# The beginning of a two-layer diffusion kernel: first three scales on TensorE, another order of loads, low parts right behind their products

## The chip, the core and the metric

One core of a Trainium2 chip runs the whole program in one launch. TensorE (PE) multiplies, VectorE (DVE), ScalarE (ACT) and GpSimd (POOL) work elementwise, SyncE (SP) issues the loads. The metric is the device time of one launch in microseconds, lower is better.

## What is computed

Three transformer blocks of width 1024 run over 256 latent and 256 context tokens, with nine condition vectors per layer made from silu(c). The change touches only the first half-FFN of the first layer, whose input is a modulated norm:

```python
def adaln(cond, w, b):
    m = jax.nn.silu(cond) @ w + b
    return m.reshape(m.shape[:-1] + (N_MOD, D_MODEL))

def modulated_norm(h, g, m, k):
    return rmsnorm(h, g) * (1.0 + m[..., k + 1, :]) + m[..., k, :]

def half_ffn(h, m, k, g_pre, g_post, w_in, w_out):
    y = swiglu(modulated_norm(h, g_pre, m, k), w_in, w_out)
    return gated_residual(h, y, g_post, m, k, 0.5)
```

Here k is 0: the shift is m[0], the scale m[1]. There are two conditions, one for the context tokens and one for the latents.

## The kernel before

Activations are held transposed: 1024 channels are 8 chunks (CH) of 128 partitions, with all 512 tokens along the free axis. Every weight product is made of three single-pass products of 512 columns (or 256): w_hi x u_hi, w_lo x u_hi and w_hi x u_lo, so weights and activations are both split in a high part (rounded to fp32r) and a low part (what the rounding left). `head` (L802) on ScalarE makes w_hi of a weight tile, `rest` (L779) on GpSimd makes w_lo, in four quarters for the tiles of the beginning. Weight tiles (128 x 1024, 512 KB) sit in a ring of 6; a new one is loaded when `tile_used` says that one has been used.

The beginning, up to the first 96 products, runs so. SyncE (L702 on) issues, in order: the transposed condition silu_t (small), h in two halves, weight tile 0, the spread condition silu_c (every partition holds both conditions, 1 MB), the small columns col, and then for each chunk c a scale tile, a shift tile (512 KB each) and the next weight tile; then tables. ScalarE (L837 on) takes silu of silu_t, squares h chunk by chunk, then in `first_norm` (L875) takes silu of silu_c, loads the table of exp and log, makes 1/rms (`rstd`) when the sum of squares is there, and for each chunk adds the bias to the shift (mcol), makes u_hi for the two halves of the tokens and a head. VectorE (L1136 on) adds up the squares, makes two small sums for a later block (lam), and in `first_norm` (L1295) does for each chunk: two dot products of the scale tile with silu_c (`dot`, L1150), a_col = (1 + scale) times gain, v = h x a_col x rstd for both halves (`v_part`), and `u_low` of the chunk before it. TensorE waits in `start_phase` (L1726): one matmul with ones for the sum of squares, then for each chunk a `shift(c)` (8 fp32 matmuls of a shift tile with the two columns of silu_t, 16 records in a trace), and `run(tile, k)`, the three products of one weight tile with chunk k, for four weight tiles and 8 chunks, 96 products in all. u_lo is waited for just before the third product of a `run`.

Two dots are junk-written to psum banks 0 and 1; shift sums are in banks 6 and 7. After the 96 products `ffn_body` goes on with pair after pair of weight tiles over all 8 chunks, and nothing in the rest of the program waits for anything of the beginning but through those products, u, and the ring.

`keep_clock(bank, count)` (L1645) issues `count` fp32 matmuls of ones with 128 columns, two records each; before the change the beginning doesn't call it, later stages do.

Of the kernel before, what the change touches and what calls it, by code (L numbers as in the profile page):

```python
# [14 lines left out]
D = 1024  # L15
# [353 lines left out]
def build(nc, A):  # L369
# [106 lines left out]
    cond_in, tables_in, consts_in, dist_in = sem("cond_in"), sem("tables_in"), sem("consts_in"), sem("dist_in")  # L476
    h_in = [sem("h_low_in"), sem("h_high_in")]
# [40 lines left out]
    FIRST_DOTS = 2 * CH  # L518
# [175 lines left out]

    def exps_through(kind, U):
        return (2 if kind == "da" else 1) * (U + 1)
# [6 lines left out]
    def _(sp):  # L703
        sp.dma_start(silu_t[:, :, :], A["cond_t"]).then_inc(cond_in, 16)
        for i in range(2):
            c = slice(4 * i, 4 * i + 4)
            sp.dma_start(h[:, c, :], A["hT"][:, c, :]).then_inc(h_in[i], 16)

# [89 lines left out]
    def _(act):  # L798
# [76 lines left out]
        def first_norm(b):  # L875
            heads_to(0)
            act.wait_ge(consts_in, 32)
            scalar.activation(silu_c[:, :, :], silu_c[:, :, :], ACT.Silu).then_inc(silu_c_ready, 1)
            scalar.preload_act_table_set(EXP_SET)
            act.wait_ge(set_up, 2)  # L880
            act.wait_ge(first_sum, CH)
# [3 lines left out]
            heads_to(1)  # L885
            for c in range(CH):
                act.wait_ge(shift_sum, c + 1)
                bias = COL["ada_b"] + c
                scalar.activation(mcol[:, :, c:c + 1], psum[:, SUMS + c % 2, 0:2].rearrange("p (c o) -> p c o", o=1),
# [4 lines left out]
                heads_to(min(c + 2, 5))  # L894
# [232 lines left out]
    def _(dve):  # L1127
# [15 lines left out]
        dve.wait_ge(consts_in, 32)  # L1143
        for m in range(2):
            l0 = COL["lambda"] + 2 * m * DA_QK
            vec.tensor_tensor_reduce(out=lam_t[:, m, :], in0=col[:, l0:l0 + DA_QK], in1=col[:, l0 + DA_QK:l0 + 2 * DA_QK],
                                     scale=1.0, scalar=0.0, op0=ALU.mult, op1=ALU.add,
                                     accum_out=small[:, 2 + m:3 + m]).then_inc(lam_sum, 1)

# [145 lines left out]
        def first_norm(b):  # L1295

            one_more, g = stat[:, 0, :], COL["norm_g"]
            bias = COL["ada_b"] + CH
            vec.tensor_scalar(one_more, col[:, bias:bias + CH], 1.0, None, ALU.add).then_inc(scale_step, 1)
            dve.wait_ge(scale_step, 1)  # L1300
            dve.wait_ge(silu_c_ready, 1)
# [287 lines left out]
    def _(pe):  # L1589
# [136 lines left out]
        def start_phase(b, tiles):  # L1726

            pe.wait_ge(silu_t_ready, 1)
            pe.wait_ge(first_sum, CH - 1)
            mm(psum[:, SUMS, :], ones[:, :], sq_first[:, CH - 1, :], start=True, stop=True).then_inc(first_sum, 1)  # L1730

            def shift(c):
                pe.wait_ge(shift_in[c], 16)
                if c == 0:
# [3 lines left out]
                for k in range(CH):  # L1738
                    last = mm(psum[:, SUMS + c % 2, 0:2], first_tile(CH + c)[:, k * 128:(k + 1) * 128], silu_t[:, k, :],
                              start=k == 0, stop=k == CH - 1)  # L1740
                last.then_inc(shift_sum, 1)
# [385 lines left out]
```

## Time and profile before

| | us |
|---|---|
| median of 3 runs (lowest, highest) | 2386.48 (2383.85, 2388.22) |
| the profiled execution, its own time | 2385.69 |
| its span, first to last instruction | 2383.9 |
| PE busy / weight loads busy | 2313.7 (97%) / 2067.1 (87%) |
| DVE / ACT / POOL busy | 1306.3 / 974.4 / 1340.7 |

Time outside the span is 1.8 us. A busy PE means that matmuls are in flight, not that the array is at its peak; PEclk is the clock granted to TensorE as a share of full speed (1.0 is 2.4 GHz, 0.5 is 1.2 GHz), and it is told as 1.00 where no record of the clock exists yet, as at the very beginning. There the duration of a matmul tells the clock. Rows of a timeline give the start, the time, the engine, the source line and what the engine waited for.

### The profile page before, as it was taken

Reading aid. Unit: us, or ns where it says so; the run is one execution under the profiler, and the core shown is the slowest. Engines: PE = TensorE matmul, PEld = TensorE weight load, DVE = VectorE, ACT = ScalarE, POOL = GpSimd, SP = SyncE. Lnnn points to the kernel's source line nnn. Section 1 sums busy time; section 2 is a strip of 40 time slices with the busy share of each in tenths; the row PEclk is TensorE's granted clock in tenths of the full one; section 3 lists DMA queues with packets and bytes.
Section 4 is the critical chain, followed back from the end, with each engine's and each line's share of the span. In section 5 each row is a group of like instructions: output and inputs, shape, how many; then the busy total and the mean of one; then the engine's idle time right before and its main releaser. Section 6 shows DMA issues by size and latency. Waiting matters only on the chain.

```text
span 2383.9 us, 36103 instructions
## 1 busy us (share of the span) xinstructions
PE 2313.7 (97%) x14528; PEld 2067.1 (87%) x14528; DVE 1306.3 (55%) x2196; ACT 974.4 (41%) x1605; POOL 1340.7 (56%) x700
## 2 busy tenths in 40 slices
PE   7999999999889999999999998999999999999998
PEld 5888889777688888898888897799999999999998
DVE  8898296666678982967332126554324315533331
ACT  4332224455443322234222235555444444555443
POOL 4554465222234554654544443278879887468886
PEclk9999999999999999999999999999999999999999
DMA  6555362211025553534453332145645564345554
GB/s 271 212 180 191 111 219 86 71 53 63 27 80 206 176 193 119 213 101 177 175 193 109 96 91 79 45 160 186 179 154 190 181 185 161 108 151 184 185 178 134
DMA packets 97508, 350.09 MB, mean 147 GB/s; under 512 B 10944, under 2 KB 10944, under 8 KB 96960
## 3 DMA queue, kind: packets, MB, share of 16 engines
q1 hardware_dynamic: 97344, 347.81, 43.6%
q8 instruction: 115, 1.88, 0.3%
q14 instruction: 49, 0.40, 0.1%
HBM read 346.71 MB, written 1.05 MB: 146 GB/s over the span
## 4 chain that ended last, share of the span: by engine, by line
PE 47%; DVE 3%; ACT 2%; POOL 1%; issue 1%; DMA 1%; DVEq 0%; ACTq 0%
PE psum L1601 15%; PE psum L1605 15%; PE psum L1602 15%; POOL w_lo L786 1%; PE psum L1950 1%; ACT w_hi L806 1%; PE psum L1922 0%; PE psum L1930 0%; DVE stat L1517 0%; PE psum L1912 0%; DVE u_lo L1457 0%; DMA w_raw<-in_ga_in 0%; ACT prob L1067 0%; DVE sbias L1508 0%; DVE psum L1233 0%
## 5 line engine op out<-in xcount | busy, mean ns | idle before, releaser
L786 POOL TENSOR_TENSOR w_lo<-w_raw,w_hi 128x1024 fp32r<-128x1024 f32 (+3 forms) x696 | 1340.5, 1948 | 1026.2 <-ACT w_hi L806 1025.6
L1601 PE MATMUL psum<-u_hi,w_hi 128*128 128x256 f32 (+2 forms) x2912 | 973.3, 334 | 11.9 <-POOL w_lo L786 7.8
L1605 PE MATMUL psum<-u_lo,w_hi 128*128 128x256 f32 (+2 forms) x2912 | 949.3, 326 | 3.8 <-DVE u_lo L1225 2.0
L1602 PE MATMUL psum<-u_hi,w_lo 128*128 128x256 f32 (+2 forms) x2912 | 946.9, 325 | 0.0
L806 ACT ACTIVATE w_hi<-w_raw 128x1024 fp32r<-128x1024 f32 (+1 forms) x522 | 537.4, 1032 | 439.2 <-PE psum L1605 345.9
L1601 PEld LDWEIGHTS psum<-u_hi,w_hi 128*128 128x128 f32 x2912 | 554.9, 191 | 75.1 <-issue 24.3
L1605 PEld LDWEIGHTS psum<-u_lo,w_hi 128*128 128x128 f32 x2912 | 554.1, 190 | 52.6 <-DVE u_lo L1225 4.9
L1602 PEld LDWEIGHTS psum<-u_hi,w_lo 128*128 128x128 f32 x2912 | 555.0, 191 | 45.9 <-issue 3.1
L1601 PE MATMUL psum<-gu_hi,w_hi 128*128 128x256 f32 (+1 forms) x1188 | 379.3, 319 | 0.1
L1602 PE MATMUL psum<-gu_hi,w_lo 128*128 128x256 f32 (+1 forms) x1188 | 378.1, 318 | 0.0
L1605 PE MATMUL psum<-gu_lo,w_hi 128*128 128x256 f32 (+1 forms) x1188 | 378.1, 318 | 0.0
L1601 PEld LDWEIGHTS psum<-gu_hi,w_hi 128*128 128x128 f32 x1188 | 226.3, 191 | 16.2 <-issue 0.5
L1602 PEld LDWEIGHTS psum<-gu_hi,w_lo 128*128 128x128 f32 x1188 | 226.3, 191 | 15.7
L1605 PEld LDWEIGHTS psum<-gu_lo,w_hi 128*128 128x128 f32 x1188 | 226.3, 191 | 15.3
L1153 DVE CUSTOM_DVE_ANT_0 psum<-ada_hi,silu_c,col 128x1024 f32<-128x1024 f32 x80 | 155.2, 1940 | 55.6 <-DMA ada_hi<-in_ada_w 52.0
L960 ACT ACTIVATE sq<-psum 128x512 f32<-128x512 f32 x66 | 39.5, 598 | 326.3 <-PE psum L1605 176.0
L1153 DVE CUSTOM_DVE_ANT_0 psum<-ada_lo,silu_c,col 128x1024 f32<-128x1024 f32 x80 | 144.9, 1812 | 30.9 <-DMA ada_lo<-in_ada_w 26.3
L1330 DVE TENSOR_TENSOR gu_lo<-sq,gu_hi 128x512 fp32r<-128x512 f32 (+1 forms) x132 | 147.4, 1117 | 17.4 <-ACT gu_hi L945 17.3
L1362 DVE TENSOR_TENSOR sq<-sq,psum 128x512 f32<-128x512 f32 (+1 forms) x110 | 63.6, 578 | 166.1 <-PE psum L1605 161.0
L1249 DVE TENSOR_TENSOR rstd<-rstd,sq 128x256 f32<-128x256 f32 (+1 forms) x58 | 46.1, 794 | 180.9 <-ACT sq L904 89.0
L1153 DVE CUSTOM_DVE_ANT_0 psum<-ada_out,silu_c,col 128x1024 f32<-128x1024 f32 x64 | 132.8, 2136 | 0.1
L1067 ACT ACTIVATE prob<-psum,stat 128x512 f32<-128x512 f32 (+1 forms) x80 | 47.6, 599 | 103.9 <-DVE stat L1519 103.8
(180 smaller groups left out, 1988.9 us busy)
## 6 DMA issues: line engine op xcount, KB each, us to landing
w_raw<-in_ffn_in SPq DMA_DIRECT2D x264, 512.0 KB, 3.5
w_raw<-in_ffn_out SPq DMA_DIRECT2D x96, 448.0 KB, 3.4
ada_hi<-in_ada_w SPq DMA_DIRECT2D x48, 512.0 KB, 5.1
ada_lo<-in_ada_w SPq DMA_DIRECT2D x48, 512.0 KB, 5.2
w_raw<-in_ffn_out SPq DMA_DIRECT2D x48, 512.0 KB, 3.6
ada_out<-in_ada_w SPq DMA_DIRECT2D x32, 512.0 KB, 3.8
w_raw<-in_b_qkv SPq DMA_DIRECT2D x30, 512.0 KB, 3.5
w_raw<-in_da_in SPq DMA_DIRECT2D x24, 512.0 KB, 3.4
```

The source lines that it names most:

```text
L786: last = pool.tensor_tensor(w_lo[:, slot, w], w_raw[:, slot, w], w_hi[:, slot, w].bitcast(F32), ALU.subtract)
L806: scalar.activation(w_hi[:, slot, 0:cols], w_raw[:, slot, 0:cols], ACT.Copy).then_inc(hi_ready, 1)
L960: scalar.activation(s_up[:, j, tok], psum[:, pair_bank(m), tok], ACT.Silu).then_inc(silu_ready, 1)
L1067: scalar.activation(prob[:, U % 2, m * 512:m * 512 + n], src, ACT.Exp, bias=stat[:, U % 4, 2 + m:3 + m], scale=scale, accum_out=stat[:, U ...
L1153: return vec.tensor_tensor_reduce(out=psum[:, junk:junk + 2, :].rearrange("p a b -> p (a b)"), in0=tile, in1=silu_c[:, c, :], scale=1.0, s ...
L1249: vec.tensor_tensor(sqsum[:, tok], sqsum[:, tok], sq[:, i % 2, tok], ALU.add).then_inc(yacc_ready, 1)
L1330: vec.tensor_tensor(gu_lo[:, m, tok], s_up[:, m % 2, tok], gu_hi[:, m, tok].bitcast(F32), ALU.subtract)\
L1362: vec.tensor_tensor(s_up[:, j, tok], s_up[:, j, tok], psum[:, pair_bank(m) + 1, tok], ALU.mult)\
L1601: mm(out, w_hi[:, slot, w], x_hi, start=start and n == 0, stop=False)
L1602: mm(out, w_lo[:, slot, w], x_hi, start=False, stop=False)
L1605: last = mm(out, w_hi[:, slot, w], x_lo, start=False, stop=stop and n == len(ks) - 1)
L1950: last = mm(psum[:, pv_bank(kind, st["s"], half), x["ocol"]:x["ocol"] + 128], v_tile(st["v"][g], kt), probT[:, U % 2, n * 128:(n + 1) * 12 ...
```

## The change

On TensorE: `start_phase` begins with 32 matmuls of `keep_clock`, sums the squares in four matmuls of pairs (with one more `keep_clock` matmul between them) in place of one, makes the scales of chunks 0, 1 and 2 with matmuls as the shifts are made (`condition`), and runs the products in another order. On VectorE: the adds of squares are four pair adds in place of a chain of seven, the dots of chunks 0 to 2 are gone (a_col is made from psum), each `u_low` stands behind the `v_part` of its own chunk, and the two dots of the next chunk stand one before and one behind it. On ScalarE: the exp table is loaded right behind the first silu and the silu table behind rstd, silu of silu_c is done in two halves behind u_hi of chunk 2, and heads come at other places. SyncE loads what the new order uses first, and silu_c behind the tiles of chunk 2. The table load at the head of the first `ffn_body` falls away. (A few lines of loads that the diff adds behind the `return` of `lag_of` are never reached.)

```diff
@@ names and constants @@
+    silu_in, first_pair, scale_sum = sem("silu_in"), sem("first_pair"), sem("scale_sum")
...
+    BY_PE = 3
+    FIRST_DOTS = 2 * (CH - BY_PE)
...
@@ SyncE: the loads @@
+        def load_scale(c):
+
+            source = A["ada_shift"][CH + c] if c < BY_PE else A["ada_w"][CH + c]
+            sp.dma_start(first_tile(c), source).then_inc(scale_in[c], 16)
+
+        def load_shift(c):
+
+            sp.dma_start(first_tile(CH + c), A["ada_shift"][c]).then_inc(shift_in[c], 16)
...
         load(A["ffn_in0"][0], 0)
-        sp.dma_start(silu_c[:, :, :], A["cond"]).then_inc(consts_in, 16)
         sp.dma_start(col[:, :], A["columns"]).then_inc(consts_in, 16)
-        for c in range(CH):
-            sp.dma_start(first_tile(c), A["ada_w"][CH + c]).then_inc(scale_in[c], 16)
-            sp.dma_start(first_tile(CH + c), A["ada_shift"][c]).then_inc(shift_in[c], 16)
-            if c + 1 < RING:
-                load(A["ffn_in0"][c + 1], c + 1)
+        for c in range(2):
+            load_scale(c)
+            load_shift(c)
+        for t in range(1, 4):
+            load(A["ffn_in0"][t], t)
+        for c in range(2, CH):
+            load_scale(c)
+            load_shift(c)
+            if c == 2:
+                sp.dma_start(silu_c[:, :, :], A["cond"]).then_inc(silu_in, 16)
+            if c > 5:
+                load(A["ffn_in0"][c - 2], c - 2)
         sp.dma_start(tab[:, :], A["tables"]).then_inc(tables_in, 16)
...
@@ ScalarE @@
         scalar.activation(silu_t[:, :, :], silu_t[:, :, :], ACT.Silu).then_inc(silu_t_ready, 1)
+        scalar.preload_act_table_set(EXP_SET)
...
             heads_to(0)
-            act.wait_ge(consts_in, 32)
-            scalar.activation(silu_c[:, :, :], silu_c[:, :, :], ACT.Silu).then_inc(silu_c_ready, 1)
-            scalar.preload_act_table_set(EXP_SET)
             act.wait_ge(set_up, 2)
-            act.wait_ge(first_sum, CH)
+            act.wait_ge(first_sum, 1)
             rstd_of(rstd[:, :], psum[:, SUMS, :], 1.0 / D, first_rstd)
             act.wait_ge(lam_sum, 2)
             scalar.activation(small[:, 4:6], small[:, 2:4], ACT.Exp).then_inc(lam_exp, 1)
-            heads_to(1)
+            scalar.preload_act_table_set(SILU_SET)
+            act.wait_ge(consts_in, 16)
             for c in range(CH):
                 act.wait_ge(shift_sum, c + 1)
                 bias = COL["ada_b"] + c
-                scalar.activation(mcol[:, :, c:c + 1], psum[:, SUMS + c % 2, 0:2].rearrange("p (c o) -> p c o", o=1),
+                scalar.activation(mcol[:, :, c:c + 1], psum[:, RSTD - c % 2, 0:2].rearrange("p (c o) -> p c o", o=1),
...
-                heads_to(min(c + 2, 5))
+                heads_to((2, 3, 3, 3, 3, 3, 4, 5)[c])
+                if c == BY_PE - 1:
+                    act.wait_ge(silu_in, 16)
+                    for i in range(2):
+                        scalar.activation(silu_c[:, i, :], silu_c[:, i, :], ACT.Silu).then_inc(silu_c_ready, 1)
...
@@ VectorE @@
-        for c in range(1, CH):
-            dve.wait_ge(first_sq, c + 1)
-            if c > 1:
-                dve.wait_ge(first_sum, c - 1)
-            total = psum[:, RSTD, :]
-            vec.tensor_tensor(sq_first[:, c, :] if c == CH - 1 else total, sq_first[:, 0, :] if c == 1 else total,
-                              sq_first[:, c, :], ALU.add).then_inc(first_sum, 1)
...
+            for x in (0, 2, 4, 6):
+                dve.wait_ge(first_sq, x + 2)
+                vec.tensor_tensor(sq_first[:, x + 1, :], sq_first[:, x, :], sq_first[:, x + 1, :], ALU.add)\
+                   .then_inc(first_pair, 1)
...
+            def scale_dot(c, i):
+
+                if c < BY_PE or c >= CH:
+                    return
+                if c == BY_PE:
+                    dve.wait_ge(silu_c_ready, i + 1)
+                dve.wait_ge(scale_in[c], 16)
+                dot(first_tile(c), i, 2 * (c - BY_PE) + i, 0, ada_sum[:, c % 2, i:i + 1], 0)
+
             for c in range(CH):
-                dve.wait_ge(scale_in[c], 16)
-                for i in range(2):
-                    dot(first_tile(c), i, 2 * c + i, 0, ada_sum[:, c % 2, i:i + 1], 0)
-                dve.wait_ge(ada_dot, 2 * c + 2 + ADA0)
-                vec.tensor_scalar(a_col[:, 0:6:3, c:c + 1], ada_sum[:, c % 2, :].rearrange("p (c o) -> p c o", o=1),
+                if c < BY_PE:
+                    dve.wait_ge(scale_sum, c + 1)
+                    scale = psum[:, c % 2, 0:2]
+                else:
+                    dve.wait_ge(ada_dot, 2 * (c - BY_PE) + 2 + ADA0)
+                    scale = ada_sum[:, c % 2, :]
+                vec.tensor_scalar(a_col[:, 0:6:3, c:c + 1], scale.rearrange("p (c o) -> p c o", o=1),
                                   one_more[:, c:c + 1], col[:, g + c:g + c + 1], ALU.add, ALU.mult)\
...
                     v_part(b, p, tok, c, rstd)
-                    if c:
-                        u_low(b, p, tok, c - 1)
-            for p, tok in enumerate(halves(FULL)):
-                u_low(b, p, tok, CH - 1)
+                scale_dot(c + 1, 0)
+                for p, tok in enumerate(halves(FULL)):
+                    u_low(b, p, tok, c)
+                scale_dot(c + 1, 1)
...
@@ TensorE @@
+            keep_clock(PVB, 32)
+            for n in range(4):
+                pe.wait_ge(first_pair, n + 1)
+                last = mm(psum[:, SUMS, :], ones[:, :], sq_first[:, 2 * n + 1, :], start=n == 0, stop=n == 3)
+                if n < 3:
+                    keep_clock(PVB, 1)
+            last.then_inc(first_sum, 1)
             pe.wait_ge(silu_t_ready, 1)
-            pe.wait_ge(first_sum, CH - 1)
-            mm(psum[:, SUMS, :], ones[:, :], sq_first[:, CH - 1, :], start=True, stop=True).then_inc(first_sum, 1)
...
+            def scale(c):
+
+                pe.wait_ge(scale_in[c], 16)
+                if c == 2:
+                    pe.wait_ge(scale_step, 2)
+                condition(first_tile(c), psum[:, c % 2, 0:2]).then_inc(scale_sum, 1)
...
+            scale(0)
             shift(0)
+            scale(1)
+            run(*tiles[0], 0)
+            shift(1)
+            scale(2)
+            run(*tiles[0], 1)
             for k in range(2):
-                shift(k + 1)
-                for tile in tiles[:2]:
-                    run(*tile, k)
+                run(*tiles[1], k)
+            shift(2)
             for k in range(2):
-                for tile in tiles[2:]:
-                    run(*tile, k)
-            for k in range(2, CH):
+                run(*tiles[2], k)
+            for tile in tiles[:3]:
+                run(*tile, 2)
+            shift(3)
+            for k in range(3):
+                run(*tiles[3], k)
+            for k in range(3, CH):
                 if k + 1 < CH:
                     shift(k + 1)
                 for tile in tiles:
...
@@ the tensors made on the host @@
-    X["ada_shift"] = I["ada_w"][0][:, 0:D].reshape(CH, 128, CH, 128).transpose(2, 1, 0, 3).reshape(CH, 128, D)
+    X["ada_shift"] = I["ada_w"][0][:, 0:D + 384].reshape(CH, 128, CH + 3, 128).transpose(2, 1, 0, 3).reshape(CH + 3, 128, D)
```

## Rows read from the trace of the kernel before

**Rows 1.** Windows: busy us (instructions) of each engine, granted clock, DMA share, GB/s.

```profile
0.00:13.23 13.23, 0.00 (x0) 0.03 (x1) 5.07 (x9) 6.82 (x11) 1.27 (x6) 1.00 0.83 324
18.19:25.02 6.83, 6.83 (x33) 6.83 (x33) 6.69 (x10) 3.02 (x5) 5.82 (x6) 1.00 1.02 408
25.02:28.79 3.77, 3.07 (x7) 1.97 (x8) 3.73 (x6) 2.23 (x4) 3.66 (x4) 1.00 1.03 412
32.06:37.05 4.99, 4.78 (x11) 3.29 (x12) 4.89 (x8) 2.23 (x4) 2.74 (x4) 1.00 1.03 410
37.05:50.80 13.75, 13.61 (x84) 11.76 (x83) 13.53 (x23) 4.11 (x10) 5.85 (x6) 1.00 0.39 156
50.80:54.20 3.40, 3.40 (x9) 2.62 (x10) 3.29 (x7) 0.37 (x1) 0.00 (x0) 0.50 0.00 0
54.20:66.47 12.27, 12.27 (x72) 10.68 (x71) 9.73 (x21) 4.67 (x9) 0.00 (x0) 1.00 0.06 15
66.47:150.00 83.53, 83.53 (x370) 69.19 (x369) 76.50 (x75) 24.00 (x32) 49.65 (x16) 1.00 0.60 214
150.00:320.00 170.00, 170.00 (x752) 140.77 (x751) 112.84 (x124) 48.22 (x61) 80.25 (x31) 1.00 0.46 161
```

**Rows 2.** Timeline of TensorE: sum of squares, shifts (L1739), products (L1601, L1602, L1605).

```profile
13.23 2.04 PE L1730 MATMUL psum<-sq_first,ones 128*128 128x512 f32 x2 [13.23 <-DVE sq_first L1141]
18.19 6.96 PE L1739 MATMUL psum<-silu_t,first_b 128*128 128x2 f32 x32 [2.92 <-ACT rstd L834]
...
26.92 0.80 PE L1605 MATMUL psum<-u_lo,w_hi 128*128 128x512 f32 x1 [0.70 <-DVE u_lo L1225]
...
28.79 3.41 PE L1739 MATMUL psum<-silu_t,first_b 128*128 128x2 f32 x16
...
35.35 0.63 PE L1601 MATMUL psum<-u_hi,w_hi 128*128 128x512 f32 x1
35.77 0.63 PE L1602 MATMUL psum<-u_hi,w_lo 128*128 128x512 f32 x1
...
38.97 1.84 PE L1739 MATMUL psum<-silu_t,first_b 128*128 128x2 f32 x16
40.67 0.47 PE L1601 MATMUL psum<-u_hi,w_hi 128*128 128x512 f32 x1
...
43.52 1.84 PE L1739 MATMUL psum<-silu_t,first_b 128*128 128x2 f32 x16
...
50.65 0.67 PE L1605 MATMUL psum<-u_lo,w_hi 128*128 128x512 f32 x1
```

**Rows 3.** Timeline of VectorE: lambda sum, dots (L1153) of chunks 2, 6 and 7.

```profile
13.48 0.23 DVE L1146 CUSTOM_DVE_ANT_0 lam_t<-col 128x64 f32<-128x64 f32 x1 [0.39 <-DMA col<-in_columns]
...
26.79 1.76 DVE L1153 CUSTOM_DVE_ANT_0 psum<-first_a,silu_c 128x1024 f32<-128x1024 f32 x1
...
50.52 1.22 DVE L1153 CUSTOM_DVE_ANT_0 psum<-first_a,silu_c 128x1024 f32<-128x1024 f32 x1
...
55.07 1.22 DVE L1153 CUSTOM_DVE_ANT_0 psum<-first_b,silu_c 128x1024 f32<-128x1024 f32 x1
```

**Rows 4.** Timeline of ScalarE: squares, silu of silu_c, rstd, mcol, u_hi.

```profile
8.95 2.19 ACT L843 ACTIVATE sq_first<-h 128x512 f32<-128x512 f32 x4 [0.38 <-DMA h<-in_hT]
...
13.48 1.91 ACT L878 ACTIVATE silu_c<-silu_c 128x2048 f32<-128x2048 f32 x1 [1.39 <-DMA col<-in_columns]
15.40 1.28 ACT L879 ACT_TABLE_LOAD   x1
16.70 0.69 ACT L826 ACTIVATE rstd<-psum,small 128x512 f32<-128x512 f32 x1
...
21.78 0.26 ACT L889 ACTIVATE mcol<-psum,col 128x2 f32<-128x2 f32 x1 [2.69 <-PE psum L1739]
22.07 0.91 ACT L872 ACTIVATE u_hi<-v,mcol 128x256 fp32r<-128x256 f32 x2
```

**Rows 5.** Timeline of TensorE much later: `keep_clock` matmuls, 12 records, two per matmul.

```profile
1569.58 1.50 PE L1648 MATMUL psum<-ones 128*128 128x128 f32 x12
```

More of the change, by code:

```diff
@@ L707, in _, with load_scale, load_shift @@
             sp.dma_start(h[:, c, :], A["hT"][:, c, :]).then_inc(h_in[i], 16)
+        def load_scale(c):
+            source = A["ada_shift"][CH + c] if c < BY_PE else A["ada_w"][CH + c]
+            sp.dma_start(first_tile(c), source).then_inc(scale_in[c], 16)
+        def load_shift(c):
+            sp.dma_start(first_tile(CH + c), A["ada_shift"][c]).then_inc(shift_in[c], 16)
         def load_ada(phase, n, slot):
@@ L725, in _ @@
         load(A["ffn_in0"][0], 0)
[L726 removed]
         sp.dma_start(col[:, :], A["columns"]).then_inc(consts_in, 16)
[L728 to L732 removed]
+        for c in range(2):
[7 more added lines that the diff above has]
+            if c == 2:
+                sp.dma_start(silu_c[:, :, :], A["cond"]).then_inc(silu_in, 16)
+            if c > 5:
+                load(A["ffn_in0"][c - 2], c - 2)
         sp.dma_start(tab[:, :], A["tables"]).then_inc(tables_in, 16)
@@ L940, in ffn_body @@
             tok, f, t0 = b["tok"], b["f"], b["t_body"]
-            scalar.preload_act_table_set(SILU_SET)
+            if b["n"]:
+                scalar.preload_act_table_set(SILU_SET)
             def gu_high(m):
@@ L1298, in first_norm @@
             bias = COL["ada_b"] + CH
-            vec.tensor_scalar(one_more, col[:, bias:bias + CH], 1.0, None, ALU.add).then_inc(scale_step, 1)
-            dve.wait_ge(scale_step, 1)
-            dve.wait_ge(silu_c_ready, 1)
-            for c in range(CH):
-                dve.wait_ge(scale_in[c], 16)
-                for i in range(2):
-                    dot(first_tile(c), i, 2 * c + i, 0, ada_sum[:, c % 2, i:i + 1], 0)
-                dve.wait_ge(ada_dot, 2 * c + 2 + ADA0)
-                vec.tensor_scalar(a_col[:, 0:6:3, c:c + 1], ada_sum[:, c % 2, :].rearrange("p (c o) -> p c o", o=1),
+            for x in (0, 2, 4, 6):
+                dve.wait_ge(first_sq, x + 2)
+                vec.tensor_tensor(sq_first[:, x + 1, :], sq_first[:, x, :], sq_first[:, x + 1, :], ALU.add)\
+                   .then_inc(first_pair, 1)
+            dve.wait_ge(consts_in, 16)
+            vec.tensor_scalar(one_more, col[:, bias:bias + CH], 1.0, None, ALU.add).then_inc(scale_step, 1)
+            for m in range(2):
+                l0 = COL["lambda"] + 2 * m * DA_QK
+                vec.tensor_tensor_reduce(out=lam_t[:, m, :], in0=col[:, l0:l0 + DA_QK], in1=col[:, l0 + DA_QK:l0 + 2 * DA_QK],
+                                         scale=1.0, scalar=0.0, op0=ALU.mult, op1=ALU.add,
+                                         accum_out=small[:, 2 + m:3 + m]).then_inc(lam_sum, 1)
+            dve.wait_ge(scale_step, 1)
+            def scale_dot(c, i):
[5 more added lines that the diff above has]
+                dot(first_tile(c), i, 2 * (c - BY_PE) + i, 0, ada_sum[:, c % 2, i:i + 1], 0)
+            for c in range(CH):
+                if c < BY_PE:
[5 more added lines that the diff above has]
+                vec.tensor_scalar(a_col[:, 0:6:3, c:c + 1], scale.rearrange("p (c o) -> p c o", o=1),
                                   one_more[:, c:c + 1], col[:, g + c:g + c + 1], ALU.add, ALU.mult)\
@@ L1726, in start_phase, with condition @@
         def start_phase(b, tiles):
-            pe.wait_ge(silu_t_ready, 1)
-            pe.wait_ge(first_sum, CH - 1)
-            mm(psum[:, SUMS, :], ones[:, :], sq_first[:, CH - 1, :], start=True, stop=True).then_inc(first_sum, 1)
+            keep_clock(PVB, 32)
[5 more added lines that the diff above has]
+            last.then_inc(first_sum, 1)
+            pe.wait_ge(silu_t_ready, 1)
+            def condition(tile, out):
+                for k in range(CH):
+                    last = mm(out, tile[:, k * 128:(k + 1) * 128], silu_t[:, k, :], start=k == 0, stop=k == CH - 1)
+                return last
+            def scale(c):
[3 more added lines that the diff above has]
+                condition(first_tile(c), psum[:, c % 2, 0:2]).then_inc(scale_sum, 1)
             def shift(c):
                 pe.wait_ge(shift_in[c], 16)
-                if c == 0:
+                if c == 1:
                     pe.wait_ge(first_rstd, 1)
@@ L1737, in shift @@
                     pe.wait_ge(shift_ready, c - 1)
[L1738 to L1741, printed above, removed]
+                condition(first_tile(CH + c), psum[:, RSTD - c % 2, 0:2]).then_inc(shift_sum, 1)
             def run(t, bank, tok, k):
```

9 lines of the change are left out of this document (2 added, 7 removed).

## The prediction

> **What bounds the kernel now.** I read the windows first, by stretch. Up to 13.23 us TensorE does nothing; from 66.47 us on it is busy without a gap, 83.53 of 83.53 us and 170.00 of 170.00 us [rows 1]. VectorE is the next busiest there, 76.50 of 83.53 us, then 112.84 of 170.00 [rows 1]. So the whole rest hangs on TensorE, and what the change is worth is how much earlier or later the 96 first products end. That end is 66.47 us; call it E. The rest moves with it one for one, as nothing there waits for a clock time.
>
> Then the timeline of TensorE up to E, to see what fills it. The sum of squares starts at 13.23, the shifts at 18.19 behind rstd, the first product at 25.02 [rows 1, 2]. Two prices come out of it. At the upper clock level (2.4 GHz) a shift takes 1.70 us (38.97 to 40.67) and the 12 products of a chunk 2.85 us (40.67 to 43.52), 0.238 each. At the lower (1.2 GHz) a shift takes 3.4 us and a product 0.43 (35.35 to 35.77) [rows 2]. At the upper level the work from 18.19 on would be 8 x 1.70 + 96 x 0.238 = 36.4 us and end at 54.6. It ends 12 us later: the engine is at the lower level until 37.05, which costs some 9 us, and again from 50.80 to 54.20 (granted 0.50), 1.7 us; the rest is idling for u_lo, such as 0.70 us before 26.92 [rows 1, 2]. **The bound of the beginning is TensorE and its clock.**
>
> What did the engine do before the clock moved? From 18.19 to 25.02 it was 6.83 of 6.83 us busy, with shifts alone (two moving columns), and stayed low. From 25.02 to 28.79 came products with a gap: still low. In 32.06 to 37.05 it had 4.78 us of dense work, nearly all products: then it rose [rows 1, 2]. It fell at 50.80, at a shift with a product held up behind it (the one at 50.65) [rows 1, 2]. So I take it that shifts don't hold the clock, and products do.
>
> **The change, part by part.**
>
> Priming. 32 keep-clock matmuls can start when `ones` are set, about 1.4 us. 12 records take 1.50 us at the upper level, so a matmul (two records) is 0.22 and about 0.44 at the lower [rows 5]. The rise comes, by the 3.4 to 5 us of dense work seen in [rows 1], between 5 and 8.4 us: the 32 end at 10.4 to 12.0; I take 11.0. All at the lower level they would end at 15.5.
>
> Sum of squares. Before: one matmul, 2.04 us at the lower level, ended at 15.27 [rows 2]. After: four, about 0.9 each at the upper, and three fillers, 4.3 us: 11.0 to 15.3. The pair adds are ready in time: the squares end at 8.95 + 2.19 = 11.14 [rows 4]. So the sum is no earlier. But rstd is: before, ScalarE was held by silu of silu_c (1.91) and a table load (1.28) and began ln at 16.70 [rows 4]. After, ln and exp run at once, 15.4 to 16.8, against 18.05.
>
> Loads. The stream moves 0.41 MB a us from start to about 42 us in either order [rows 1]. Counting 512 KB a tile from the end of h at 8.95 [rows 4]: scale 0 lands at 12.2, shift 0 at 13.5, scale 1 at 14.8, shift 1 at 16.0, weight tiles 1 to 3 by 19.9, scale 2 at 21.1, silu_c at 25.0, scale 3 at 26.3, weight tiles 4 and 5 at 36.5 and 40.3. Each is there before its user in the schedule below, so the order of loads costs nothing and gives nothing by itself. The silu_c load moved past 11 others on SP's queue has its cover in ScalarE, which wants it at 36 us. If that cover were gone, VectorE's dots of chunk 3 would wait.
>
> Scales on TensorE. Six dots leave VectorE, 1.22 us each, up to 1.76 beside GpSimd [rows 3]. They were only partly on the path. Three scales come to TensorE, on the path: 5.1 us at the upper level, 10.2 at the lower. And scale 0, shift 0, scale 1 form 5.1 us in which no product runs, where by [rows 1, 2] the clock falls again.
>
> Low parts. For chunks 3 to 7 VectorE has what it had: a chunk is 4.55 us (50.52 to 55.07 [rows 3]), as long as TensorE's 1.70 + 2.85. The new wait is at chunk 2: `u_low(2)` is queued on VectorE behind the first dot of chunk 3, which waits for silu of silu_c, which ScalarE makes behind u_hi of chunk 2. TensorE waits for u_low(2) in the third product of tile 0. From the end of shift(2): mcol 0.3, u_hi 0.9, half of the silu 1.0 (half of 1.91) [rows 4], dot 1.3, u_low 0.8, together some 4.4 us with semaphores, against 8 products of 1.9 us: 2.5 us idle, or 1 us at the lower clock.
>
> Covered: the table loads (ScalarE idles 2.69 us and more before each mcol [rows 4]); heads and low parts of tiles 4 and 5 (1.0 and about 3.7 us, four quarters in [rows 1], against 8.5 us of products between u_hi of chunk 7 and the first use of tile 5). If that cover were gone the next pair would wait a few us.
>
> The sum, likeliest course, in us from the span's start:
> - 15.3 scale 0, 17.0 shift 0, 18.7 scale 1, in which the clock falls: 21.3
> - 3 products at the lower level 22.6, shift 1 26.0, scale 2 29.4, 9 products 33.3; the clock comes back at their end
> - shift 2 35.0, 8 products 36.9, idle to 39.4; here the clock falls again, as at 50.80 before, where the hold-up was shorter
> - 7 products 42.4, shift 3 45.8, 9 products of tile 3 49.6, shift 4 53.0: all low. Chunk 3: 8 products low 56.4, the clock rises, 4 more 57.4
> - shifts 5 to 7 and chunks 4 to 7: 5.1 + 11.4 = 16.5: **E = 73.9**
>
> That is 7.4 us later than 66.47. The profiled execution took 2385.69 us, span 2383.9 and 1.8 around it; 2385.69 + 7.4 = 2393.1, taken as 2393.0. That execution is 0.8 us under the median shown, well inside the runs' own spread of 4.4 us, so I shift nothing.
>
> On the page TensorE: Matmul & The Clock Gate of the Trainium skill (Why this matters for your kernels): a TensorE kept busy continuously reaches the full clock, and only idle gaps take it back. The trace disagrees for shifts: wholly busy from 18.19 to 25.02, and no rise [rows 1]. By the page's rule E would be that of the first rival.
>
> **The rivals.**
> - *The clock stays up* from the priming on, as a busy engine holds it. Then 15.3 + 11 x 1.70 + 22.8 + 2.5 idle = 59.3, 7.2 us less: 2378.5, faster. For it: once at the upper level, single shifts of 1.70 were mostly survived (37.05 to 50.80 at 1.00 [rows 1]). Against it: the 6.83 us of shifts without a rise, and the fall at 50.80. It decides when three such blocks in a row don't bring the clock down. Chance 0.10.
> - *The clock returns early and holds*: in the first 9 products, and the idle at chunk 2 doesn't take it for long. From 39.4: 7 products 1.7, five shifts 8.5, 9 + 60 products 16.4: E = 66.0. If it only comes back in tile 3's products, E = 70.3. That is 2385 to 2389.5, no change. For it: 3.84 us of gapless products at the lower level is near what raised it before 37.05. Chance 0.33.
> - *The clock doesn't return in the first 9 products.* Shift 2 at 3.4, everything low until chunk 3: E = 75.6, or 79.5 if it rises only in chunk 4: 2395 to 2399. For it: the 3.77 us with a gap that did not raise it [rows 1]. Chance 0.17.
> - *The priming doesn't do what it says*, the clock is still low at its end: the sum ends at 25 and not 15.3, and scale 0 and shift 0 cost 3.4 more: about 13 us above the likeliest, 2406. Chance 0.03.
>
> The likeliest course has 0.37. **Range** 2384 to 2399: the three middle cases, less their tails.
>
> A measurement of this kernel tells about 0.2%, 4.8 us, from no change: under 2381.7 is faster, over 2391.3 slower. Faster is the first rival, 0.10. Slower: 0.30 of the likeliest's 0.37 (its end moves by some 2 us with where the clock turns), 0.17 and 0.03: 0.50. Same: 0.33 and 0.07, 0.40.
>
> **What would show it.** In the timeline after: the keep-clock records fall to 0.11 apart before 8.4 us; the sum ends near 15.3; rstd near 16.8; the records of scale 1 or shift 1 double in time (granted clock 0.50 near 20 us); the first product starts near 21.3; an idle time of 1 to 2.5 us before a product with u_lo in chunk 2, ended by VectorE, followed by a second low stretch; E near 74. The forecast is wrong if the granted clock is 1.00 through the scales and shifts, if the stretch with TensorE gapless begins later or earlier by something else than E (for instance a wait for weight tile 5), or if the chunks from 4 on take clearly more than 4.55 us.

## The result, and the profile after

The changed kernel takes 2391.57 us (median of 19 runs, 2387.87 to 2397.9) against 2386.48 (19 runs, 2383.16 to 2392.09). The ratio is 1.0022, 95% interval 1.0016 to 1.0029: 4 to 7 us slower. Its profiled execution has a span of 2390.3 us, 6.4 more than before.

Windows of the kernel after (columns as in [rows 1]); from 20.08 to 73.90 they are cut where its granted clock turns:

```profile
15.16:20.77 5.61, 5.61 (x49) 5.61 (x48) 2.05 (x5) 4.54 (x8) 0.00 (x0) 0.94 1.02 407
20.08:33.73 13.65, 13.65 (x54) 12.49 (x54) 5.79 (x10) 4.02 (x7) 8.87 (x12) 0.50 1.02 411
33.73:40.56 6.83, 4.55 (x25) 3.55 (x26) 3.21 (x6) 3.07 (x5) 0.00 (x0) 1.00 1.03 410
40.56:57.63 17.07, 17.07 (x59) 14.76 (x58) 11.25 (x24) 2.34 (x6) 0.00 (x0) 0.50 0.10 41
57.63:73.90 16.27, 16.27 (x95) 14.26 (x96) 13.36 (x26) 6.48 (x13) 6.75 (x6) 1.00 0.05 11
74.00:160.00 86.00, 86.00 (x381) 71.23 (x380) 79.11 (x80) 25.56 (x35) 51.35 (x19) 1.00 0.60 212
```

TensorE is as busy as an engine can be in four of the first five, and yet it stands at half its clock in 30.7 us of them (13.65 + 17.07). Before, it was some 19 us up to 37.05, as the durations in [rows 2] tell, and 3.4 from 50.80 [rows 1]. The stretch without a gap, 66.47 to 320 in [rows 1], now begins at 73.92 us.

The timeline of TensorE, kernel after, with what answers to [rows 2]:

```profile
1.45 9.77 PE L1687 MATMUL psum<-ones 128*128 128x128 f32 x64 [1.45 <-DVE small L1165]
...
14.30 1.02 PE L1770 MATMUL psum<-sq_first,ones 128*128 128x512 f32 x2
15.16 1.84 PE L1779 MATMUL psum<-silu_t,first_a 128*128 128x2 f32 x16
16.87 1.93 PE L1779 MATMUL psum<-silu_t,first_b 128*128 128x2 f32 x16
18.65 2.26 PE L1779 MATMUL psum<-silu_t,first_a 128*128 128x2 f32 x16
20.77 0.77 PE L1640 MATMUL psum<-u_hi,w_hi 128*128 128x512 f32 x1
...
22.20 3.41 PE L1779 MATMUL psum<-silu_t,first_b 128*128 128x2 f32 x16
25.47 3.55 PE L1779 MATMUL psum<-silu_t,first_a 128*128 128x2 f32 x16
28.88 0.77 PE L1640 MATMUL psum<-u_hi,w_hi 128*128 128x512 f32 x1
...
39.44 0.50 PE L1644 MATMUL psum<-u_lo,w_hi 128*128 128x512 f32 x1 [2.28 <-DVE u_lo L1243]
...
73.69 0.39 PE L1644 MATMUL psum<-u_lo,w_hi 128*128 128x512 f32 x1
```

The priming (the 32 matmuls at the start) is over at 11.06, and the first product starts at 20.77, 4.2 us sooner than the 25.02 of [rows 1]. But a block of shifts or scales that takes 1.84 at 15.16 takes 3.41 and 3.55 at 22.20 and 25.47, and TensorE waits 2.28 us for a low part of chunk 2; the text below calls this the hold-up. The 96 products end with the record that starts at 73.69.

ScalarE and VectorE at the two places that decide, kernel after:

```profile
15.43 0.69 ACT L854 ACTIVATE rstd<-psum,small 128x512 f32<-128x512 f32 x1 [3.52 <-PE psum L1770]
...
36.28 1.99 ACT L925 ACTIVATE silu_c<-silu_c 128x1024 f32<-128x1024 f32 x2
```

```profile
37.35 1.23 DVE L1171 CUSTOM_DVE_ANT_0 psum<-first_a,silu_c 128x1024 f32<-128x1024 f32 x1 [6.23 <-ACT silu_c L925]
38.50 0.14 DVE L1171 DVE_READ_ACCUMULATOR2_ANT ada_sum<- 128x1 f32 x1
38.50 0.88 DVE L1243 SCALAR_TENSOR_TENSOR u_lo<-v,mcol,u_hi 128x256 fp32r<-128x256 f32 x2
```

rstd starts at 15.43, not 16.70 as in [rows 4]. VectorE idles 6.23 us for silu of silu_c, then does the dot, and only then the low part that TensorE waits for.

### The profile page after: what moved, and what is told of

It is laid out like the page before. It is cut to its first block, busy times and chain, and to the rows that moved or that the text cites. A ratio compares the mean times of both kernels' runs of the same rounds, so it can differ in the third digit from the quotient of the medians.

```text
span 2390.3 us, 36335 instructions
## 1 busy us (share of the span) xinstructions
PE 2333.8 (98%) x14652; PEld 2087.2 (87%) x14652; DVE 1297.9 (54%) x2181; ACT 974.2 (41%) x1606; POOL 1330.6 (56%) x700
## 4 chain that ended last, share of the span: by engine, by line
PE 61%; DVE 4%; ACT 2%; POOL 1%; DMA 1%; issue 1%; DVEq 0%; SPq 0%; ACTq 0%
PE psum L1640 19%; PE psum L1644 19%; PE psum L1641 19%; POOL w_lo L814 1%; PE psum L2014 1%; ACT w_hi L834 1%; PE psum L1986 0%; PE psum L1994 0%; DVE stat L1556 0%; DVE h L1257 0%; PE psum L1976 0%; DVE psum L1251 0%; DVE u_lo L1496 0%; DMA w_raw<-in_ffn_in 0%; DMA w_raw<-in_ga_in 0%
## 5 line engine op out<-in xcount | busy, mean ns | idle before, releaser
L1401 DVE TENSOR_TENSOR sq<-sq,psum 128x512 f32<-128x512 f32 (+1 forms) x110 | 63.7, 579 | 160.1 <-PE psum L1644 155.0
L1171 DVE CUSTOM_DVE_ANT_0 psum<-ada_out,silu_c,col 128x1024 f32<-128x1024 f32 x64 | 140.4, 2256 | 0.1
L1267 DVE TENSOR_TENSOR rstd<-rstd,sq 128x256 f32<-128x256 f32 (+1 forms) x58 | 39.1, 675 | 180.0 <-ACT sq L935 87.6
```

The lines of the kernel that those rows point to most:

```text
L1171: return vec.tensor_tensor_reduce(out=psum[:, junk:junk + 2, :].rearrange("p a b -> p (a b)"), in0=tile, in1=silu_c[:, c, :], scale=1.0, s ...
L1267: vec.tensor_tensor(sqsum[:, tok], sqsum[:, tok], sq[:, i % 2, tok], ALU.add).then_inc(yacc_ready, 1)
L1401: vec.tensor_tensor(s_up[:, j, tok], s_up[:, j, tok], psum[:, pair_bank(m) + 1, tok], ALU.mult)\
```

## The experiments

Twelve kernels ran, all against runs of the kernel before on the same chip. "End" is the end of the 96 first products in the profiled execution: 66.5 us before, 73.9 after. "Low" is the time up to that end at a granted clock of 0.50, or, where it says "to", up to the first record of the clock. In the kernels with priming that record comes between 4.7 and 7.1 us, and the time before it is left out.

| kernel | median us | ratio to before (95%) | end us | low, us |
|---|---|---|---|---|
| after | 2391.57 | 1.0022 (1.0016 to 1.0029) | 73.9 | 20.1 to 33.7, 40.6 to 57.6 |
| a_wide | 2382.41 | 0.9981 (0.9972 to 0.9989) | 59.3 | none from 4.8 |
| a_early | 2385.51 | 0.9995 (0.9987 to 1.0004) | 66.9 | 20.7 to 41.2 |
| a_order | 2385.00 | 0.9996 (0.9988 to 1.0005) | 63.9 | 19.7 to 33.3 |
| a_first3 | 2387.73 | 1.0004 (0.9995 to 1.0013) | 63.7 | 25.6 to 39.3 |
| a_loads | 2391.77 | 1.0016 (1.0007 to 1.0025) | 73.8 | 19.7 to 33.4, 40.2 to 57.3 |
| a_noprime | 2395.08 | 1.0031 (1.0021 to 1.0042) | 73.5 | to 12.8, 19.6 to 33.2, 40.1 to 57.1 |
| b_prime | 2389.38 | 1.0011 (1.0003 to 1.0020) | 64.9 | 16.1 to 36.6 |
| b_wide | 2385.98 | 0.9996 (0.9987 to 1.0005) | 64.5 | to 21.4, 28.2 to 31.6 |
| b_prime_wide | 2387.25 | 1.0003 (0.9994 to 1.0012) | 64.8 | 27.3 to 30.7 |
| a_wide_early | 2378.31 | 0.9963 (0.9949 to 0.9976) | 57.5 | none from 5.4 |
| a_wide_early_np | 2379.51 | 0.9969 (0.9958 to 0.9981) | 58.1 | to 13.7 |
| a_wide_early_22 | 2376.45 | 0.9957 (0.9944 to 0.9969) | 56.6 | none from 4.7 |

Names with a_ start from the kernel after, with b_ from the kernel before.

**Is it the clock?** The theory of the prediction is that blocks of shifts and scales, which move two columns a matmul, let the clock fall, and that this is the loss. A block is the 8 matmuls of one shift or scale; with two columns it is called narrow here. The rival: three more blocks on TensorE are too much whatever the clock. a_wide gives these matmuls 128 columns, the same two 64 times over, and reads the first two.

```diff
-                    last = mm(out, tile[:, k * 128:(k + 1) * 128], silu_t[:, k, :], start=k == 0, stop=k == CH - 1)
+                    last = mm(out.rearrange("p (a b) -> p a b", b=2), tile[:, k * 128:(k + 1) * 128],
+                              silu_t[:, k, :].unsqueeze(1).to_broadcast([128, 64, 2]), start=k == 0, stop=k == CH - 1)
```

> The changed kernel, with each scale and shift matmul moving 128 columns (the two of the condition, 64 times over) in place of 2; the sums are read from the first two as before. Nothing else differs. Clock theory (the blocks without products let the clock fall, and that is the loss): no granted clock under 1.0 up to the end of the 96 products except perhaps at the hold-up in chunk 2, blocks of 1.8 us each in place of 1.7 to 3.4, the 96 products end at 59 to 62 us in place of 73.9, and the kernel takes 2377 to 2380 us, faster than both. Rival, the three scales are too much work for TensorE or the order of the products is bad whatever the clock: the end stays over 66 us and the kernel over 2386. Rival, wide columns cost time of their own: blocks take over 2 us each and the gain is under 5 us.

Windows and timeline of TensorE, a_wide:

```profile
15.10:59.30 44.20, 41.82 (x268) 36.82 (x268) 34.12 (x67) 19.45 (x37) 16.05 (x18) 1.00 0.65 258
```

```profile
16.16 1.95 PE L1779 MATMUL psum<-silu_t,first_b 128*128 128x128 f32 x16
17.95 1.95 PE L1779 MATMUL psum<-silu_t,first_a 128*128 128x128 f32 x16
...
32.74 0.50 PE L1644 MATMUL psum<-u_lo,w_hi 128*128 128x512 f32 x1 [2.27 <-DVE u_lo L1243]
```

The clock is 1.00 from its first record at 4.8 us to the end, a block takes 1.79 us (16.16 to 17.95), 0.09 more than the 1.70 of a narrow one, and the end comes at 59.3, 14.7 us sooner than after. The work on TensorE is the same as in the kernel after, so the clock is shown to be the loss, and the rival falls. The time, 2382.4, is 2.4 above the range expected: of 14.7 us in the two ends the medians give back some 10 (ratios 1.0022 and 0.9981). The two profiled spans differ by 12.3, as what lies behind the end took 2318.8 us here and 2316.4 after; the section on the prediction comes back to this. The page TensorE: Matmul & The Clock Gate of the Trainium skill (Why this matters for your kernels) has a busy TensorE keep its clock. Here TensorE was 13.65 of 13.65 us busy at 0.50 after, and stayed at 1.00 with the same instructions made wider, so the measurement decides against "busy" as the condition.

**Which blocks?** a_first3 is wide in scale 0, shift 0 and scale 1 alone.

```diff
-                condition(first_tile(c), psum[:, c % 2, 0:2]).then_inc(scale_sum, 1)
+                condition(first_tile(c), c % 2, c < 2).then_inc(scale_sum, 1)
...
-                condition(first_tile(CH + c), psum[:, RSTD - c % 2, 0:2]).then_inc(shift_sum, 1)
+                condition(first_tile(CH + c), RSTD - c % 2, c == 0).then_inc(shift_sum, 1)
```

> The changed kernel with wide columns in the first three blocks alone (scale 0, shift 0, scale 1); all later scales and shifts move 2 columns, the silu of silu_c is where the change has it. It tells whether the first three blocks in a row are what brings the clock down. If they are: the granted clock stays 1.0 to the hold-up at 30 us at least, and the 96 products end at 59 to 64 us, the kernel 2380 to 2385. If shift 1 and scale 2, with three products ahead of them, do it as well: a low stretch begins between 23 and 27 us, the end is at 65 to 70, the kernel 2386 to 2390.

```profile
5.10:25.60 20.50, 20.24 (x151) 17.87 (x151) 9.06 (x21) 13.28 (x23) 7.77 (x11) 1.00 1.02 413
25.60:39.30 13.70, 13.01 (x42) 10.56 (x41) 6.63 (x13) 3.08 (x5) 4.37 (x6) 0.50 1.03 410
```

The fall at 20 us is gone and another comes at 25.6, with shift 1 and scale 2 just behind. So the first three blocks bring it down, and two blocks in a row behind three products do it as well. Single narrow blocks mostly don't: after, the ones at 62.07 and 66.64, each between groups of twelve products, left the clock at 1.00. In the kernel before it did fall once, at 50.80, behind a single one at 48.09 and 0.14 us of idle time before the product at 50.65. The end, 63.7, lies under the 65 to 70 that I expected for this case, since only one low stretch is left and not two; the time, 2387.7, lies in its range. The hold-up falls into that low stretch and is 0.69 us there, so this run says nothing on what a hold-up at full clock does.

**Is the hold-up in chunk 2 behind the second low stretch?** a_early and a_order take it away in two ways. The first moves the silu, the second the dot.

```diff
-                if c == BY_PE - 1:
+                if c == BY_PE - 2:
                     act.wait_ge(silu_in, 16)
```

```diff
-                scale_dot(c + 1, 0)
+                if c + 1 != BY_PE:
+                    scale_dot(c + 1, 0)
                 for p, tok in enumerate(halves(FULL)):
                     u_low(b, p, tok, c)
+                if c + 1 == BY_PE:
+                    scale_dot(c + 1, 0)
                 scale_dot(c + 1, 1)
```

> The changed kernel, with the silu of silu_c behind u_hi of chunk 1 instead of chunk 2 (silu_c has landed by 25 us). It takes away the 2.3 us hold-up of TensorE at u_lo of chunk 2. If the hold-up is what brought the clock down a second time: the low stretch from 40 to 57 us is gone or much shorter, and the kernel is 4 to 8 us faster than the changed one, 2384 to 2388. If the shifts alone bring it down, as around 20 us, only the idle time itself is saved: 0 to 3 us, 2389 to 2392.

> The changed kernel with VectorE's first dot of chunk 3 behind, not ahead of, u_low of chunk 2; the silu of silu_c stays where the change has it. TensorE then has u_lo of chunk 2 at 37.1 us in place of 39.4. If the place of that dot is the cause of the hold-up and of the second fall of the clock: as with the early silu, the idle time is gone, the low stretch from 40 to 57 us too or mostly, end of the 96 products at 65 to 70 us, the kernel 2383 to 2388. If the second fall has another cause: only 2.3 us are saved, end at 71 to 72, 2389.

The windows of a_order, and of a_early:

```profile
19.70:33.30 13.60, 13.60 (x54) 12.44 (x54) 5.59 (x10) 4.21 (x7) 8.86 (x12) 0.50 1.02 411
33.30:63.90 30.60, 30.38 (x179) 25.98 (x180) 26.84 (x52) 11.99 (x24) 6.11 (x6) 1.00 0.33 126
```

```profile
20.70:41.20 20.50, 20.50 (x74) 18.28 (x74) 10.44 (x19) 6.77 (x11) 9.12 (x12) 0.50 1.03 411
41.20:66.90 25.70, 25.70 (x154) 22.56 (x154) 22.29 (x45) 8.95 (x19) 6.81 (x6) 1.00 0.08 26
```

In both, the clock doesn't fall a second time, and the end is 10.0 and 7.1 us sooner for a hold-up of 2.3. a_order's end, 63.9, is even under the 65 to 70 that I expected; a_early named no end. Both medians are some 6 us under the kernel after and can't be told from the kernel before. a_early came back from its first low stretch only at 41.2, not at 33.7, though TensorE ran the same matmuls at the same times, to 0.1 us, from 20.77 to 32.86 in both. So one profile doesn't tell how long a stretch lasts, and the difference between the two ends is no measure of the two edits. It also makes a_early the weaker witness, as its clock was still low where the hold-up had been. The clean one is a_order, whose clock was up there and stayed up; against it stand the kernel after, a_loads and a_noprime, which have the hold-up and fell at 40.1 to 40.6. The hold-up alone isn't enough either: in a_wide it is there, 2.27 us, and the clock stays. It takes the hold-up together with narrow blocks around it.

**The other parts.** a_loads puts one weight tile behind each scale and shift again; a_noprime leaves out the 32 matmuls.

```diff
-        for c in range(2):
-            load_scale(c)
-            load_shift(c)
-        for t in range(1, 4):
-            load(A["ffn_in0"][t], t)
-        for c in range(2, CH):
+        for c in range(CH):
             load_scale(c)
             load_shift(c)
             if c == 2:
                 sp.dma_start(silu_c[:, :, :], A["cond"]).then_inc(silu_in, 16)
-            if c > 5:
-                load(A["ffn_in0"][c - 2], c - 2)
+            if c + 1 < RING:
+                load(A["ffn_in0"][c + 1], c + 1)
```

> The changed kernel with a weight tile loaded behind the scale and shift tile of each chunk 0 to 4, as before the change; silu_c still behind chunk 2. Theory: every tile still lands before its user, so nothing moves: end of the 96 products within 1.5 us of 73.9, the kernel 2390 to 2393. Rival, the order of loads matters: more than 3 us either way, with an idle time ended by a DMA.

```diff
-            keep_clock(PVB, 32)
             for n in range(4):
                 pe.wait_ge(first_pair, n + 1)
```

> The changed kernel without its first 32 keep-clock matmuls; the fillers between the four sums stay. Theory: the priming bought almost nothing, since its clock is lost again by 20 us; the sum ends 0 to 2 us later, the clock may still rise in the sums, and the 96 products end at 73 to 77 us, the kernel within 3 us of the changed one (2390 to 2395). Rival, the priming carries the beginning: everything is 9 to 13 us later, 2400 to 2405.

Who waited for whom on TensorE up to the end, a_loads:

```profile
PE psum L1639 <- DVE u_lo L1238: 2.3, 1, 2.3
PE psum L1682 <- DVE small L1160: 1.4, 1, 1.4
```

No wait for a DMA, the same end (73.8) and the same time: the order of loads does nothing in this schedule. The priming does as little for the end. Without it the sums raise the clock by themselves:

```profile
8.49 2.04 PE L1769 MATMUL psum<-sq_first,ones 128*128 128x512 f32 x2 [8.49 <-DVE sq_first L1319]
...
13.92 1.02 PE L1769 MATMUL psum<-sq_first,ones 128*128 128x512 f32 x2
14.78 1.84 PE L1778 MATMUL psum<-silu_t,first_a 128*128 128x2 f32 x16
```

A sum takes 2.04 us at 8.49 and 1.02 at 13.92, and scale 0 starts at 14.78, earlier than the 15.16 with priming (I had expected 0 to 2 us later), since the 32 matmuls held TensorE to 11.06 with the first pair sum ready at 8.2. The profiled span is nevertheless 6.1 us longer than after; that comes later in the program (below). Its ratio overlaps that of the kernel after, so a cost of leaving the priming out is not shown; the median, 2395.1, is at the upper edge of the 2390 to 2395 expected.

**The same edits on the kernel before.** b_prime adds the 32 matmuls, b_wide only the wide columns, b_prime_wide both, with 40 matmuls ahead of the sum and 18 behind it.

```diff
+            keep_clock(PVB, 40)
             pe.wait_ge(silu_t_ready, 1)
             pe.wait_ge(first_sum, CH - 1)
             mm(psum[:, SUMS, :], ones[:, :], sq_first[:, CH - 1, :], start=True, stop=True).then_inc(first_sum, 1)
+            keep_clock(PVB, 18)
...
-                    last = mm(psum[:, SUMS + c % 2, 0:2], first_tile(CH + c)[:, k * 128:(k + 1) * 128], silu_t[:, k, :],
-                              start=k == 0, stop=k == CH - 1)
+                    last = mm(psum[:, SUMS + c % 2, 0:128].rearrange("p (a b) -> p a b", b=2), first_tile(CH + c)[:, k * 128:(k + 1) * 128],
+                              silu_t[:, k, :].unsqueeze(1).to_broadcast([128, 64, 2]), start=k == 0, stop=k == CH - 1)
```

> The kernel before, with only the 32 keep-clock matmuls ahead of the sum of squares. Theory: the clock that they bring is lost again in the idle time until rstd and the two shifts behind it; shifts 0 and 1 take up to 3.4 us less, but the first third product waits for VectorE at 26.9 us as before. The 96 products end at 64 to 67 us and the kernel is 0 to 3 us faster than before, not told from it. Rival, a clock raised early is worth its half of the 19 us at the lower level: end at 57 to 60, 7 to 9 us faster.

> The kernel before with nothing changed but the width of its shift matmuls, 128 columns in place of 2; no priming. Theory: shifts 0 and 1 now raise the clock at 22 to 25 us in place of 37, but VectorE, which has no idle time from 15.5 to 59.6 us, paces what follows: the end of the 96 products at 62 to 65 in place of 66.5, the kernel 1 to 4 us faster than before. Rival, the lower clock until 37 us is what costs: end under 60 us, 7 us faster or more.

> The kernel before, with 40 keep-clock matmuls ahead of the sum of squares, 18 behind it (so that TensorE doesn't idle until rstd) and shift matmuls of 128 moving columns. No scale on TensorE, order of loads and of VectorE as before. Theory: the clock stays up, but VectorE, which idles nowhere from 15.5 to 59.6 us before, then sets the pace: the 96 products end at 62 to 64 us in place of 66.5 and the kernel takes 2382 to 2384. Rival, the clock is all there is: the end comes at 56 to 58 us and the kernel takes 2376 to 2378, as fast as or faster than the changed kernel with wide columns, and the scales on TensorE are worth nothing.

Windows of b_prime, then TensorE's waits and a window in b_prime_wide:

```profile
16.10:36.60 20.50, 17.64 (x64) 15.16 (x65) 20.11 (x30) 9.38 (x17) 15.19 (x14) 0.50 1.03 409
```

```profile
PE psum L1605 <- DVE u_lo L1225: 6.7, 3, 3.9
```

```profile
15.50:60.00 44.50, 37.46 (x231) 32.22 (x230) 43.10 (x70) 16.46 (x33) 20.70 (x20) 0.96 0.62 248
```

Priming alone is lost at 16.1, in the idle time before rstd. Its end moved by 1.6 us as expected, but the median is 0.03 to 0.20% above before, not under it: a miss, with its reason behind the end (below). With wide columns the clock is up but for 3.4 us, and now TensorE waits 6.7 us for low parts, with VectorE busy 43.10 of 44.50 us. So in the kernel before VectorE stands right behind the clock. b_wide ends at 64.5, within the 62 to 65 expected, and b_prime_wide at 64.8, 0.8 later than expected; neither median can be told from the kernel before, and that of b_prime_wide, 2387.25, is 3 us above its range of 2382 to 2384. Against them a_wide ends 5.2 and 5.5 us sooner. That is about what the scales on TensorE and the rest of the change are worth once the clock is up, though each of the two still has one low stretch of 3.4 us.

**A version that beats both.** a_wide_early has both edits, a_wide_early_22 also 22 matmuls in place of 32, a_wide_early_np none.

```diff
-            keep_clock(PVB, 32)
+            keep_clock(PVB, 22)
```

> The changed kernel with both edits: scale and shift matmuls of 128 moving columns, and the silu of silu_c behind u_hi of chunk 1. Theory: with the clock up, the hold-up in chunk 2 costs only its idle time, 2.3 us. The 96 products end at 57 to 58 us in place of 59.3, the kernel takes 2379 to 2381, 1 to 3 us less than with wide columns alone. Rival, VectorE's chain of 4.55 us a chunk from the first dot of chunk 3 sets the end: also 57 to 58, but with TensorE idle before u_lo in chunks 4 to 7. Rival, the idle time only moves on to another wait: 59.3 again, 2382.

> Wide columns and early silu as in the run before, and 22 keep-clock matmuls at the start in place of 32. With the clock up and no hold-up left, TensorE is busy from the sum of squares to the end of the 96 products, so a sum that starts earlier moves everything: the priming ends at 8.8 to 9.5 us in place of 11.1, the last sum waits for the last pair add at 11.7 and ends near 13, and the 96 products end at 55 to 56 in place of 57.5: 2376 to 2377, 2 us less. Rival, something else is next (scale 2 or silu_c not landed, rstd): the end stays over 57 us.

> The same with no keep-clock matmuls at the start at all (the three fillers between the sums stay). Theory: the sums themselves raise the clock at 12 to 15 us and the wide blocks hold it, so the 96 products end at 57 to 60 us, 0 to 2 us later than with 32 and 2 to 4 later than with 22: 2378 to 2381. Rival, without priming the clock is low well into the scales: the end comes over 62 us.

The waits of TensorE up to the end, in a_wide_early and then in a_wide_early_22:

```profile
PE psum L1644 <- DVE u_lo L1243: 0.3, 1, 0.3
```

```profile
PE psum L1779 <- DMA first_a<-in_ada_shift: 1.5, 1, 1.5
```

With the hold-up down to 0.26 us (at 31.00, in chunk 2) the end is at 57.5, and TensorE doesn't idle before low parts in chunks 4 to 7, so it is TensorE and not VectorE's chain that sets it; the median, 2378.3, is 0.7 under its range. The 22 matmuls start the sums at 8.31 in place of 10.55, 2.2 us sooner, and 1.0 us of it arrives: scale 2, which lands at 22.3, is next and TensorE waits 1.46 us for it. That is the rival of that run, in part: the end, 56.6, is later than the 55 to 56 expected. Two kernels above had waited for a load too, but shortly: a_first3 for 0.26 us, b_prime_wide for 0.33. The lowest median is 2376.45 us, 0.43% under the kernel before, though its interval overlaps that of a_wide_early. Without priming it is 58.1 and 2379.5, as expected.

## Why the prediction was right

The forecast was 2393.0 us, with 2384 to 2399; the time is 2391.57, slower as forecast.

| step | forecast, us | profile after |
|---|---|---|
| priming ends | 10.4 to 12.0, taken 11.0 | 11.06 |
| sum of squares ends | 15.3 | 15.16, scale 0 starts |
| rstd made, against 18.05 | 15.4 to 16.8 | 15.43 to 16.78 |
| clock falls, in scale 1 | 18.7 to 21.3 | 20.08 |
| first product | 21.3 | 20.77 |
| clock back | 33.3 | 33.73 |
| idle for u_lo of chunk 2 | to 39.4, 2.5 us | to 39.44, 2.28 us |
| clock falls again | there | 40.56 |
| clock back, in chunk 3 | 56.4 | 57.63 |
| 96 products end | 73.9 | 73.92 |

*The clock.* That shifts don't hold it was the step on which all hung, read from 6.83 busy us without a rise [rows 1]. a_wide shows it: same order and waits, no fall. The rival that the clock stays up had its price right (59.3, a_wide ends at 59.3) and its condition wrong.

*The hold-up at chunk 2.* Its mechanism, the dot queued ahead of the low part behind a late silu, stands in the VectorE lines above. a_order and a_early show what it costs: not its 2.3 us but a second low stretch. What I had not seen is that it does so only beside narrow blocks. The forecast had the clock back after 8 of the 12 products of chunk 3; in the profile all 12 were slow (52.14 to 57.41).

*Priming, loads.* The forecast gave the loads nothing and the priming no earlier sum. a_loads and a_noprime agree for the end, 73.8 and 73.5.

*VectorE.* Dots leaving VectorE were called "only partly on the path". That holds after, where TensorE is the bound. b_prime_wide shows that in the kernel before VectorE was close behind: it stops the end at 64.8.

*The size.* This is the term that was off. I let the rest of the program move one for one with the end: 2393.0 is 6.5 us over the median before, and 5.1 were measured. In the two profiles the end moved by 7.4 and the span by 6.4. What lies behind the end took 2317.4 us before and 2316.4 after, and it isn't constant from kernel to kernel: it goes from 2316.4 to 2322.9 in these profiles.

The record has the span and the mean granted clock of every run, and they tell what moves there. An estimate: one minus the mean clock, times the span, is the time lost to low stretches; from it goes half of the time at 0.50 up to the end in that kernel's profile. What is left, per run, is 4.5 us after (19 runs) and 5.7 to 6.7 before (34, 28 and 22 runs), 9.1 in a_wide, 9.7 in b_prime. Mean time minus end lies between 2317.6 and 2324.6 us over the twelve experiments, after and before; with this loss taken off too it lies between 2313.0 and 2315.8. So the term that was put as constant is the time lost to low stretches outside those of the profiled beginning. It makes up 1.2 to 2.2 of the 2.3 us by which the end overstates the difference of the medians, and most of why a_wide gives back 10 us and not 14.7. The mean clock doesn't tell where in a run they lie.

That the end of 73.9 agrees to a tenth is luck in part. The second low stretch began 1.2 us later than the forecast's 39.4 and ended 1.2 later than its 56.4, after a first product 0.5 early; and where the clock turns moved by 7.5 us between a_early and the kernel after. From run to run it moves too: one run of a_noprime took 2387.27 us at a mean clock of 0.995, which is some 24 us at 0.50 in the whole program, less than the 30.7 of its profile's beginning alone. The 19 runs after are spread over 10 us, and those before over 8.9. The slow ones have the lower clock: 2397.9 us at 0.989, 2390.0 on average for the six runs at 0.993.

## What to carry to other kernels

A TensorE that is busy all the time can still stand at half clock: look at the granted clock and at how long the same instruction takes, stretch by stretch, before work is moved to it. The matmuls with two moving columns, during which weight loads were busy all the time (6.83 of 6.83 us from 18.19 [rows 1]), could be made 128 columns wide for almost nothing (1.79 us in place of 1.70 a block), and that held the clock where priming ahead of them didn't. And an operation put in a queue ahead of the one that TensorE waits for costs more than its own time when the clock goes with it.

## What the runs showed of the hardware that I had not expected

The rest of the program, which no experiment touches, has low stretches of 3.4 us in differing number. They follow stages in which TensorE has idle time (in a_noprime 7.94 of 10.60 us busy from 422.00 to 432.60, 5.87 of 8.00 from 647.00 to 655.00), though it is nearly always busy inside them. In a_noprime there are six behind the 96 products, four of them here:

```profile
432.60:436.00 3.40, 3.40 (x18) 3.40 (x18) 2.70 (x7) 2.00 (x6) 0.00 (x0) 0.50 0.00 0
654.50:657.90 3.40, 3.40 (x12) 2.90 (x12) 1.28 (x5) 0.38 (x1) 0.00 (x0) 0.50 0.00 0
675.00:678.40 3.40, 3.40 (x18) 3.40 (x17) 2.10 (x2) 0.00 (x0) 1.42 (x1) 0.50 0.00 0
...
1784.30:1787.70 3.40, 3.36 (x16) 3.13 (x15) 3.40 (x11) 2.25 (x6) 0.00 (x0) 0.50 0.00 0
```

The kernel after has two, and its rest takes 2316.4 us against 2322.9. b_prime has five and takes 2321.0, a_first3 six and 2321.6, a_early two and 2316.5. b_prime_wide breaks the order a little, two and 2319.2. Over all fourteen profiles, with a stretch of 6.8 us counted as two, each goes with about 1.0 us more (correlation 0.81).

The same kernel has more or fewer from one execution to the next: of the 34 runs of the kernel before beside a_wide, the 10 with a mean clock of 0.995 took 2388.5 us on average and the 7 with 0.998 took 2385.3. But not all of it is chance. By the estimate above b_prime loses 9.7 us a run outside the low stretch of its profiled beginning, and the kernel before 5.7 to 6.7. These 3 to 4 us are about what its median lies above the time that its earlier end made me expect. Why b_prime should have more of them than the kernel before, or a_wide more than after, no run shows. A change of some us in this kernel is thus told by medians over many runs, with the mean clock beside them, and a single profile is good for the stretch that was changed, not for the whole.
